# Hybrid attention, GLA and Hyena block, fp32 on one core: the adaLN projection leaves the weight ring

## The chip, the cores and the metric

One of the eight cores of a Trainium2 chip runs the kernel. The metric is the time of one execution on the device in microseconds (us); the median of three runs stands for a kernel. TensorE is the matrix engine, VectorE and ScalarE the elementwise engines, GpSimd (POOL) and SyncE (SP) mostly issue DMAs here. The page of the profile calls them PE, DVE, ACT, POOL and SP.

## The reference

Two layers of a diffusion backbone in fp32, 256 latent and 256 context tokens, width 1024. What bears on this case is how a layer gets its modulation: from a conditioning vector (c for the latents, c_ctx for the context) six vectors of 1024 are made, with a weight w_ada of 1024 x 6144 per layer and a bias b_ada:

```
mod = silu(c) @ w_ada[layer] + b_ada[layer]        # for c and for c_ctx
shift1, scale1, gate1, shift2, scale2, gate2 = split(mod, 6)
h   = layer_norm(x) * (1 + scale1) + shift1
y   = token_mixer(h)                    # differential attention, GLA, Hyena, gates, output projection
x   = layer_norm(ALPHA * x + gate1 * y) * ln1_g + ln1_b
h   = layer_norm(x) * (1 + scale2) + shift2
x   = layer_norm(ALPHA * x + gate2 * conv_ffn(h)) * ln2_g + ln2_b
```

Layer 1, the last, needs the context only as keys, values and GLA state, so its gate1, shift2, scale2 and gate2 are wanted for the latents alone. Only the latents are put out.

## The kernel before, in words

All weights pass through one ring of four buffers (NBUF): SP loads a chunk of 512 KB (256 rows of K by 512 columns) into `stage` (L517 to L521), ScalarE rounds it to `w_hi` (L1073), VectorE makes `w_lo`, the rest (L1418), and TensorE multiplies three times with operands of 128x128 by up to 512 columns in the fp32r format: hi by hi, lo by hi, hi by lo (`three`, L696). The split runs AHEAD = 3 chunks in front of TensorE's use. A chunk has 24 matmuls in most groups.

The order of all this is one list of steps written by `plan()` (L158). Each engine walks through the same list and does its part of each step, so each engine's queue is in that order. A `group` is a projection in 1, 2, 4 or 11 chunks (a_q, a_k, a_v, three of hy, g_v, g_qk, z, six of gate, g_r, six of branch, two of out, two of down); other steps (an attention unit, a Hyena or GLA piece) are put between its chunks from lists of slots. The up projection is a hardware loop of 11 times four chunks.

The adaLN projection is a set of groups too (turn "A"): 12 per layer, each 512 columns wide with four chunks. Its stationary operand is `ada_c`, 128 columns of which four are used: silu(c) and silu(c_ctx), each as hi and lo; so a chunk has four matmuls of 128x128 by 512 columns (`ada_chunk`, L744). The first four groups of layer 0 (shift1, scale1) are the first thing that the kernel does; the other eight of layer 0 lie between the chunks of g_r, gate and branch (2 ada chunks after each); the twelve of layer 1 lie in the down projection of layer 0 (3, later 2 after each). ScalarE copies the four rows of a finished group to `mod_row` (L1170), POOL writes them to DRAM (`d_mod`), and reads them back as rows of 128 (`modload`), VectorE adds hi, lo and bias (L1474, L1475), TensorE turns them to columns (`modcols`, L761), and ScalarE copies them out, so that `modulate` (L1150) can use them as per-partition scale and bias. The gates are written to DRAM once more (`d_gate`) and broadcast from there to all 128 partitions (`gate_rows`, POOL), for the residual (L1608).

At the start ScalarE's queue issues the loads of x, VectorE makes the moments of the layer norm, ScalarE normalises (L1136), TensorE transposes (L772), and ScalarE and VectorE modulate and split the result to `h_hi` and `h_lo`.

The attention mix has one unit per chunk (`attend`, from hy on): TensorE scores, VectorE the maxima (L1666), ScalarE the exponentials (L1263), VectorE the reciprocals and the difference of the two maps (L1670 to L1673), TensorE the transposes (L886) and the product with the values. After four units come `head_norm` and a transpose (`y_turn`, L905). Banks 0 to 3 of PSUM belong to the chunks of a group, banks 4 to 7 to what lies between.

Of the kernel before, what the change touches and what calls it, by code (L numbers as in the profile page):

```python
# [14 lines left out]
P = 128  # L26
D = 1024
# [91 lines left out]
ADA_GROUPS = (range(0, 4), range(4, 12))  # L119
# [23 lines left out]
class Group:  # L143


    def __init__(self, kind, layer, index, turn, n_chunks, tiles, bank0=0, pair=False):
# [4 lines left out]
        self.late = pair or kind in ("a_q", "a_k", "a_v", "hy", "g_v", "g_qk") or self.key == ("ada", 0, 3)  # L151
# [3 lines left out]

def plan():  # L158
# [14 lines left out]
    def ada(layer, groups, bank0=4):  # L173

        out = []
        for i in groups:
            g = Group("ada", layer, i, "A", 4, [i % 2], bank0)
            out += [[("chunk", g, j)] for j in range(4)]
            out[-1].append(("evac", g))
        return out  # L180

    def spread(slots, chunks, first, per):

        for n, item in enumerate(chunks):
            slots[first + n // per] += item

    steps += [("start",), ("modbias", 0, 0)]
    slots = ada(0, ADA_GROUPS[0])
    for tt in range(4):
        slots[9 + tt].append(("moments", 0, 0, tt))  # L190
    steps += sum(slots, [])
    steps += [("modload", 0, 0), ("params", 0)]
    steps += [("deviation", 0, 0, tt) for tt in range(4)] + [("normal", 0, 0, tt) for tt in range(4)]
    steps += [("turn", 0, 0, 0), ("modcols", 0, 0), ("turn", 0, 0, 1)]
    steps += [("modulate", 0, 0, s, b) for b in range(4) for s in range(2)]
    for layer in range(DEPTH):
# [4 lines left out]
        if last:  # L201
            filt[0] += [("modulate", layer, 0, 0, b) for b in range(4)]
            filt[8].append(("modcols", layer, 1))
        else:
            filt[1].append(("consts",))
# [37 lines left out]
        for tt in qt:  # L243
            mix += [[("gla_out", layer, tt)]]
        for j in range(5):
            group("gate", layer, j, "F", 4, range(4), mix)
# [6 lines left out]
        if not last:  # L253
            slots[0].append(("modbias", layer, 1))
            spread(slots, ada(layer, ADA_GROUPS[1]), 0, 2)
            slots[15].append(("modload", layer, 1))

# [9 lines left out]
        slots = [[], [("modcols", layer, 1)] if not last else [], [("gate_rows", layer, 0)], [],  # L267
# [6 lines left out]
        slots[8] += [("gate_rows", layer, 1), ("residual", layer, 1)]  # L274
        if not last:

            slots[0].append(("modbias", layer + 1, 0))
            spread(slots, ada(layer + 1, range(0, 8)), 0, 3)
            slots[6].append(("modload", layer + 1, 0))
            slots[8].append(("modcols", layer + 1, 0))  # L280
# [1610 lines left out]
```

## Time and profile before

| | |
|---|---|
| three runs | 1848.07, 1854.63, 1859.21 us; median 1854.63 |
| profiled execution, first to last instruction (span) | 1850.7 us, of the same size as the runs |
| TensorE busy | 1657.6 us (90%) |
| VectorE busy | 1055.1 us (57%) |
| ScalarE busy | 866.0 us (47%) |
| granted clock of TensorE, mean | 0.946 of 2.4 GHz |
| loads of w_ada | 96 of 512 KB, of 252 MB in all |

The span has no measured part around it, so the profiled execution is compared by its span. How to read the rows: "busy" is the union of an engine's instructions in the stretch, "(x...)" their count; PEclk is the clock that TensorE was granted, 1.00 for 2.4 GHz and 0.50 for 1.2 GHz. Matmuls overlap: a row gives 0.39 us for one of 128x128 by 512 columns, while the next starts much earlier, so the distance of two starts is the price of one in a row of them. "[2.27 <-DVE w_lo L1418]" says that the engine had been idle for 2.27 us until that instruction's result came. Operands are named as out<-moving,stationary. An fp32 matmul (not fp32r) stands in the trace as two records.

### The profile page before, as it was taken

What the parts mean: (1) busy time and instruction counts of PE and PEld (TensorE: products, weight loads), DVE (VectorE), ACT (ScalarE), POOL (GpSimd) and SP (SyncE); (2) the same over time, 40 slices, a digit from 0 to 9 for tenths busy, and PEclk for the clock granted to TensorE, in tenths of its full rate; (3) what the DMA queues carried; (4) which work ended last, traced back from release to release, by engine and by line L of the source; (5) the groups of instructions that cost most, each with busy time, mean ns of one, the idle gap of its engine ahead of it and who ended that gap; (6) DMA issues with size and microseconds to landing.
All of it is one profiled execution on the core that took longest, in us unless ns stands there. A gap on an engine that the chain in (4) does not pass through costs nothing. (4 is left out here: it accounts for less than half of the span.)

```text
span 1850.7 us, 23144 instructions
## 1 busy us (share of the span) xinstructions
PE 1657.6 (90%) x8523; PEld 1364.9 (74%) x8523; DVE 1055.1 (57%) x1609; ACT 866.0 (47%) x1242; POOL 106.9 (6%) x204
## 2 busy tenths in 40 slices
PE   5899899999799996999999989599898878879995
PEld 3777667777687775788887767477786777769984
DVE  6545663523364668566566554865634345778864
ACT  5524543155355424545545434634534644457741
POOL 0200000000001110000000000300000001100000
PEclk8899999999789998999999989799899989989998
DMA  8422113233146772322335856422232335745572
GB/s 307 135 68 80 58 46 91 70 102 103 47 144 221 255 260 91 103 91 91 91 107 179 292 191 211 143 88 73 92 114 80 114 92 173 243 134 181 187 241 68
DMA packets 147909, 252.46 MB, mean 136 GB/s; under 512 B 11842, under 2 KB 59900, under 8 KB 147568
## 3 DMA queue, kind: packets, MB, share of 16 engines
q1 hardware_dynamic: 135472, 216.77, 37.1%
q0 software_dynamic: 11776, 32.45, 5.2%
q10 hardware_dynamic: 576, 2.10, 0.3%
q8 instruction: 55, 0.90, 0.2%
q14 instruction: 30, 0.25, 0.0%
HBM read 235.28 MB, written 15.99 MB: 136 GB/s over the span
## 5 line engine op out<-in xcount | busy, mean ns | idle before, releaser
L1418 DVE TENSOR_TENSOR w_lo<-stage,w_hi 128x1024 fp32r<-128x1024 f32 x302 | 362.4, 1222 | 342.6 <-ACT w_hi L1073 341.1
L689 PE MATMUL ps<-h_hi,w_hi 128*128 128x512 f32 (+1 forms) x1360 | 472.4, 347 | 8.4 <-ACT sig L1220 4.7
L689 PE MATMUL ps<-h_lo,w_hi 128*128 128x512 f32 (+1 forms) x1360 | 462.7, 340 | 0.0
L689 PE MATMUL ps<-h_hi,w_lo 128*128 128x512 f32 (+1 forms) x1360 | 462.7, 340 | 0.0
L1073 ACT ACTIVATE w_hi<-stage 128x1024 fp32r<-128x1024 f32 x302 | 312.6, 1055 | 315.0 <-PE ps L689 243.4
L689 PEld LDWEIGHTS ps<-h_hi,w_hi 128*128 128x128 f32 x1360 | 261.3, 192 | 41.9 <-issue 8.2
L689 PEld LDWEIGHTS ps<-h_hi,w_lo 128*128 128x128 f32 x1360 | 261.3, 192 | 27.6 <-issue 0.7
L689 PEld LDWEIGHTS ps<-h_lo,w_hi 128*128 128x128 f32 x1360 | 260.8, 192 | 28.0
L689 PE MATMUL ps<-w_hi,h_hi 128*128 128x512 f32 x384 | 156.0, 406 | 9.6 <-DVE w_lo L1418 4.3
L1819 DVE TENSOR_TENSOR w_lo<-stage,w_hi 128x1024 fp32r<-128x1024 f32 x88 | 104.5, 1223 | 86.1 <-ACT w_hi L1367 85.4
L689 PE MATMUL ps<-w_lo,h_hi 128*128 128x512 f32 x384 | 152.8, 398 | 0.0
L689 PE MATMUL ps<-w_hi,h_lo 128*128 128x512 f32 x384 | 152.8, 398 | 0.0
L1367 ACT ACTIVATE w_hi<-stage 128x1024 fp32r<-128x1024 f32 x88 | 89.1, 1052 | 76.9 <-PE ps L689 74.5
L689 PE MATMUL ps<-w_hi,act_hi 128*128 128x512 f32 x264 | 106.5, 403 | 4.1 <-DVE ffn_t L1832 3.3
L1832 DVE SCALAR_TENSOR_TENSOR ffn_t<-ps,pcol,ffn_t 128x510 f32<-128x510 f32 (+1 forms) x176 | 95.7, 609 | 25.1 <-ACT ffn_t L1374 23.9
L689 PE MATMUL ps<-w_hi,act_lo 128*128 128x512 f32 x264 | 105.7, 400 | 0.0
L689 PE MATMUL ps<-w_lo,act_hi 128*128 128x512 f32 x264 | 105.5, 400 | 0.0
L689 PE MATMUL ps<-w_hi,ada_c 128*128 128x512 f32 x192 | 83.1, 433 | 22.7 <-DVE w_lo L1418 22.7
L689 PEld LDWEIGHTS ps<-w_hi,h_hi 128*128 128x128 f32 x384 | 74.3, 193 | 31.2 <-issue 8.7
L689 PEld LDWEIGHTS ps<-w_lo,h_hi 128*128 128x128 f32 x384 | 73.9, 192 | 16.0
L689 PEld LDWEIGHTS ps<-w_hi,h_lo 128*128 128x128 f32 x384 | 74.1, 193 | 15.4 <-issue 0.5
L689 PE MATMUL ps<-w_lo,ada_c 128*128 128x512 f32 x192 | 80.6, 420 | 0.0
(262 smaller groups left out, 2124.9 us busy)
## 6 DMA issues: line engine op xcount, KB each, us to landing
stage<-in_w_in SPq DMA_DIRECT2D x122, 512.0 KB
stage<-in_w_ada SPq DMA_DIRECT2D x96, 512.0 KB
stage<-in_ffn_w_up SPq DMA_DIRECT2D x176, 256.0 KB
stage<-in_ffn_w_down SPq DMA_DIRECT2D x44, 512.0 KB
stage<-in_w_branch SPq DMA_DIRECT2D x24, 512.0 KB
stage<-in_w_out SPq DMA_DIRECT2D x16, 512.0 KB
d_sig<-sig POOLq DMA_DIRECT2D x24, 256.0 KB, 3.1
sig_in<-d_sig POOLq DMA_DIRECT2D x24, 256.0 KB, 5.3
```

What stands on the lines that cost most here:

```text
L689: return pe.matmul(out_, lhsT, rhs, start=start, stop=stop, skip_group_check=True)
L1073: act.activation(w_hi[:, s, :], stage[:, s, :], ACT.Copy).then_inc(sem("hi_ready"), 1)
L1367: act.activation(w_hi[:, s, :], stage[:, s, :], ACT.Copy).then_inc(sem("hi_ready"), 1)
L1418: dve.tensor_tensor(w_lo[:, s, :], stage[:, s, :], w_hi[:, s, :].bitcast(F32), ALU.subtract)\
L1819: dve.tensor_tensor(w_lo[:, s, :], stage[:, s, :], w_hi[:, s, :].bitcast(F32), ALU.subtract)\
L1832: dve.scalar_tensor_tensor(out=dst[:, :, to], in0=src[:, :, of], scalar=col, in1=dst[:, :, to], op0=ALU.mult, op1=ALU.add)\
```

## The change

The adaLN projection no longer goes through the ring.

- Layer 0's shift1 and scale1: SP loads all of their weight (8 x 2 tiles of 128 x 1024, 8 MB) into SBUF that is free at the start, and TensorE multiplies in plain fp32 with the weight as the stationary operand and two columns (silu(c), silu(c_ctx)) as the moving one: 128 matmuls (`first_ada`), six of eight K steps ahead of the first half of the transposes, the other two behind it. VectorE adds the bias (`first_mod`). The first two weight chunks are split (`presplit`) just ahead of the modulation.
- The other 20 groups (8 of layer 0, 12 of layer 1): per K tile a load of 128 x 512 (256 KB, SP's queue) into a ring of four tiles, and on VectorE one multiply-accumulate per vector (`ada`): `acc += w * c[k]` with a per-partition scalar; two vectors, but one for layer 1 from group 4 on. 160 tiles. Then TensorE sums over the partitions by fp32 matmuls with a column of ones and adds the bias with the identity (`ada_sum`), and ScalarE copies the columns (`ada_cols`).
- `with_ada` puts these steps into the list by chunk number: five runs, from chunk 9 at 1.75 tiles per chunk, from 43 at 1.3, from 125 at 1.5, from 160 at 1.75, from 187 at 1.1. Without the ada groups the chunks are: a_q, a_k, a_v 0 to 11, hy 12 to 23, g_v, g_qk, z 24 to 32, gate 33 to 52, g_r 53, gate 57, branch 61, out 73 to 80, up 81 to 124, down 125 to 146, and layer 1 in the same order from 147 on. SP waits, ahead of a tile's load, for the use of the tile four before.
- Gate rows: VectorE multiplies the identity by the gate's columns (`diag`, 128 x 1024), TensorE multiplies it by a matrix of ones (two fp32 matmuls of 512 columns), and ScalarE copies the two banks.
- DRAM is out of all this: `d_mod` and `d_gate` go, and POOL's steps with them. In layer 1 dft and idft are loaded again (the ring of tiles has used their place). The conditioning vectors and b_ada come in as one set of rows.

```diff
+ADA_RUNS = ([(0, q) for q in range(4, 9)], [(0, 9), (0, 10), (0, 11), (1, 0)], [(1, q) for q in range(1, 4)],
+            [(1, q) for q in range(4, 8)], [(1, q) for q in range(8, 12)])
+ADA_SLOTS = ((9, 1.75), (43, 1.3), (125, 1.5), (160, 1.75), (187, 1.1))
+ADA_RING = 4
...
+def with_ada(steps):
+    begin, finish, n = {}, {}, 0
+    for run, groups in enumerate(ADA_RUNS):
+        first, per = ADA_SLOTS[run]
+        for i, (layer, q, k) in enumerate([(*who, k) for who in groups for k in range(KT)]):
+            c = first + int(i / per)
+            early = 80 if run == 2 else first
+            at_ = early if i < ADA_RING else c + 4
+            begin.setdefault(at_, []).extend(([("ada_open", run)] if i == 0 else []) + [("ada_load", n)])
+            finish.setdefault(c, []).append(("ada", n))
+            if k == KT - 1:
+                begin.setdefault(c + 1, []).extend([("ada_sum", layer, q), ("ada_cols", layer, q)])
+            n += 1
...
-    steps += [("start",), ("modbias", 0, 0)]
-    slots = ada(0, ADA_GROUPS[0])
...
+    steps += [("first_ada", k) for k in range(6)] + [("turn", 0, 0, 0)] + [("first_ada", k) for k in range(6, KT)]
+    steps += [("first_mod",), ("turn", 0, 0, 1), ("presplit",)]
...
+                elif st[0] == "ada_load":
+                    n = st[1]
+                    layer, q, k = ada_who(n)
+                    if n >= ADA_RING:
+                        sp.wait_ge(sem("ada_done"), at("ada_done", *ada_who(n - ADA_RING)))
+                    sp.dma_start(ada_tile(n), A["w_ada"][layer, k * P:(k + 1) * P, q * COLS:(q + 1) * COLS])\
+                        .then_inc(sem(f"ada_in{n % ADA_RING}"), 16)
...
+            def first_ada(k):
...
+                cv = c_act[:].rearrange("p (v k) -> p k v", v=2)[:, k, :]
+                for w in (1, 0):
...
+                    for n in range(KT):
+                        o = 2 * (w * KT + n)
+                        ins = mm(ps[:, 3, o:o + 2], src[:, n * P:(n + 1) * P], cv, start=(k, w, n) == (0, 1, 0), stop=k == KT - 1)
...
+            def ada_sum(layer, q):
+                b = ada_bank(layer, q)
+                pe.wait_ge(sem("ada_done"), at("ada_done", layer, q, KT - 1))
+                claim(b)
+                acc_ = ada_acc(ADA_ORDER.index((layer, q)))
+                for v in ada_vecs(layer, q):
+                    for n in range(4):
+                        mm(ps[:, b, 4 * v + n:4 * v + n + 1], acc_[:, v, n * P:(n + 1) * P], ones[:, 0:1], start=(v, n) == (0, 0), stop=False)
+                    ins = mm(ps[:, b, 4 * v:4 * v + 4], ident[:], b_col[:, layer, q // 2, q % 2 * 4:q % 2 * 4 + 4], start=False)
+                full(ins, b, "ada", layer, q)
+
+            def gate_rows(layer, which, v):
+                pe.wait_ge(sem("diag"), at("diag", layer, which, v))
+                for half in range(2):
+                    b = 4 + 2 * v + half
+                    claim(b)
+                    full(mm(ps[:, b, :], ones[:], diag[which][:, 4 * half:4 * half + 4, :].rearrange("p k n -> p (k n)")),
+                         b, "gates", layer, which, v)
...
+            def ada(n):
+                layer, q, k = ada_who(n)
+                m, w = n // KT, ada_tile(n)
+                dve.wait_ge(sem(f"ada_in{n % ADA_RING}"), 16 * (n // ADA_RING + 1))
...
+                for v in ada_vecs(layer, q):
+                    col, acc_ = c_act[:, KT * v + k:KT * v + k + 1], ada_acc(m)[:, v, :]
+                    if k == 0:
+                        ins = dve.tensor_scalar(acc_, w, col, None, ALU.mult)
+                    else:
+                        ins = dve.scalar_tensor_tensor(out=acc_, in0=w, scalar=col, in1=acc_, op0=ALU.mult, op1=ALU.add)
+                do(ins, "ada_done", layer, q, k)
```

## Rows read from the trace of the kernel before

**Rows 1.** The page, parts 1 and 5: busy us by engine; the split on VectorE, mean ns.
```profile
PE 1657.6 (90%) x8523; PEld 1364.9 (74%) x8523; DVE 1055.1 (57%) x1609; ACT 866.0 (47%) x1242; POOL 106.9 (6%) x204
...
L1418 DVE TENSOR_TENSOR w_lo<-stage,w_hi 128x1024 fp32r<-128x1024 f32 x302 | 362.4, 1222 | 342.6 <-ACT w_hi L1073 341.1
```

**Rows 2.** Busy time by stretch: span, its length, engines' busy us, clock, DMA share, GB/s.
```profile
0.00:57.45 57.45, 31.48 (x98) 22.48 (x99) 32.90 (x52) 32.09 (x41) 10.76 (x25) 0.76 0.81 276
161.00:272.00 111.00, 102.59 (x492) 77.45 (x491) 72.91 (x134) 55.78 (x108) 0.00 (x0) 0.97 0.20 60
...
513.90:672.30 158.40, 149.11 (x625) 118.71 (x625) 101.65 (x119) 75.68 (x94) 20.31 (x38) 0.96 0.65 213
...
976.00:1168.30 192.30, 178.00 (x742) 141.23 (x740) 106.96 (x112) 82.34 (x94) 10.43 (x20) 0.96 0.64 215
1269.00:1331.00 62.00, 51.43 (x340) 42.12 (x339) 44.00 (x79) 32.89 (x63) 0.00 (x0) 0.92 0.27 77
```

**Rows 3.** Timeline of TensorE: start us, own length; eight matmuls apart, then five.
```profile
528.75 0.39 PE L689 MATMUL ps<-w_hi,ada_c 128*128 128x512 f32 x1
...
530.56 0.39 PE L689 MATMUL ps<-w_hi,h_hi 128*128 128x512 f32 x1
...
1024.78 0.40 PE L689 MATMUL ps<-w_hi,act_hi 128*128 128x512 f32 x1
...
1025.95 0.40 PE L689 MATMUL ps<-w_lo,act_hi 128*128 128x512 f32 x1
```

**Rows 4.** Stretches, the instructions that touch ada_c alone (four matmuls per chunk).
```profile
513.90:672.30 158.40, 34.67 (x128) 24.32 (x128) 0.00 (x0) 0.00 (x0) 0.96 0.65 213
976.00:1168.30 192.30, 48.75 (x192) 37.03 (x192) 0.00 (x0) 0.00 (x0) 0.96 0.64 215
```

**Rows 5.** Timeline of TensorE in the down projection of layer 0.
```profile
1057.91 0.79 PE L689 MATMUL ps<-w_hi,ada_c 128*128 128x512 f32 x1 [2.27 <-DVE w_lo L1418]
...
1071.62 0.31 PE L761 MATMUL ps<-ident,mrows 32*128 32x32 f32 x1 [9.27 <-DVE mrows L1475]
```

**Rows 6.** Groups by shape (busy, mean ns), then the timeline: fp32 matmuls on TensorE.
```profile
L689 PE MATMUL ps<-v_tok,attT 128*128 128x128 f32 x160 | 21.8, 275 | 1.4 <-DVE y_tok L1691 1.4
...
160.66 0.61 PE L689 MATMUL ps<-v_tok,attT 128*128 128x128 f32 x4
...
111.00 3.17 PE L689 MATMUL ps<-f_sd,dft 128*128 128x512 f32 x7
```

**Rows 7.** Timeline of VectorE: a dependent pair and the next, independent one.
```profile
163.82 0.74 DVE L1523 SCALAR_TENSOR_TENSOR x0T<-ps,pcol,x0T 128x510 f32<-128x510 f32 x1
164.60 0.75 DVE L1526 SCALAR_TENSOR_TENSOR x0T<-ps,pcol,x0T 128x510 f32<-128x510 f32 x1
165.26 0.74 DVE L1523 SCALAR_TENSOR_TENSOR x0T<-ps,pcol,x0T 128x510 f32<-128x510 f32 x1
```

**Rows 8.** Waits of VectorE in 161 to 272 us: total, times, longest.
```profile
DVE soft L1670 <- ACT probs L1263: 18.0, 13, 1.6
DVE soft L1666 <- PE ps L689: 13.1, 5, 7.7
```

**Rows 9.** Waits of VectorE in 1266 to 1340 us, the longest.
```profile
DVE soft L1670 <- ACT probs L1263: 12.7, 8, 1.6
```

**Rows 10.** Timeline of the start: last w_ada chunk, transposes, first matmul of a_q.
```profile
34.54 1.06 ACT L1073 ACTIVATE w_hi<-stage 128x1024 fp32r<-128x1024 f32 x1 [1.42 <-DMA stage<-in_w_ada]
...
48.32 3.65 PE L772 MATMUL ps<-ident,xn_mix 128*128 128x128 f32 x16 [5.09 <-ACT xn_mix L1136]
...
57.45 0.47 PE L689 MATMUL ps<-w_hi,h_hi 128*128 128x512 f32 x1 [0.30 <-issue]
```

**Rows 11.** Stretches, all engines: GLA output products, and transposes ahead of a_q.
```profile
508.00:511.40 3.40, 3.40 (x34) 3.40 (x32) 1.53 (x3) 0.56 (x1) 0.00 (x0) 0.50 0.00 0
511.40:514.85 3.45, 3.45 (x22) 3.02 (x20) 2.57 (x6) 0.63 (x3) 0.00 (x0) 0.50 0.00 0
...
54.06:57.46 3.40, 3.10 (x16) 2.72 (x14) 2.21 (x4) 2.92 (x6) 3.40 (x8) 0.50 0.61 81
```

More of the change, by code:

```diff
@@ L171, in group @@
             steps.extend(between.pop(0))
[L173 to L185, printed above, removed]
-    steps += [("start",), ("modbias", 0, 0)]
-    slots = ada(0, ADA_GROUPS[0])
[L189 to L192, printed above, removed]
+    steps += [("start",)]
+    steps += [("moments", 0, 0, tt) for tt in range(4)]
+    steps += [("params", 0)]
     steps += [("deviation", 0, 0, tt) for tt in range(4)] + [("normal", 0, 0, tt) for tt in range(4)]
-    steps += [("turn", 0, 0, 0), ("modcols", 0, 0), ("turn", 0, 0, 1)]
+    steps += [("first_ada", k) for k in range(6)] + [("turn", 0, 0, 0)] + [("first_ada", k) for k in range(6, KT)]
+    steps += [("first_mod",), ("turn", 0, 0, 1), ("presplit",)]
     steps += [("modulate", 0, 0, s, b) for b in range(4) for s in range(2)]
@@ L244, in plan @@
             mix += [[("gla_out", layer, tt)]]
+        if last:
+            mix += [[] for _ in range(20 - len(mix))]
         for j in range(5):
@@ L642, in chunk @@
                         dma(sig_in[:, n, o:TOK], d_sig[g.layer][8 * br + 4 * half + n, :, o:TOK], f"sig_in{n}", g.layer, g.index)
-            def gate_rows(layer, which):
-                what = ("branch", layer, (1, 2)) if which == 0 else ("base", "up end", layer)
-                pool.wait_ge(sem("bank_full3"), at("bank_full3", *what))
-                pool.wait_ge(sem("gate_out"), 16 * at("gate_out", layer))
-                for s in range(tok0(layer) // SEQ, 2):
-                    v = 1 - s
-                    dma(R[which]["g"][:, v, :], bc(d_gate[layer][v, 3 * which * D:(3 * which + 1) * D], D), f"gates_in{s}", layer, which)
             def post(layer, which, tt):
@@ L807, in chunk @@
                                         h_hi[:, k, :], h_lo[:, k, :], k == 0, k == KT - 1)
-                    for kk in range(2 if g.turn not in "AZ" else 0):
+                    for kk in range(2 if g.turn != "Z" else 0):
                         k = 2 * j + kk
@@ L1457, in params_turn, with gate_rows @@
+            def gate_rows(layer, which, v):
+                for q in (4 + 6 * which, 5 + 6 * which):
+                    freed(ada_bank(layer, q), "ada", layer, q)
+                if v:
+                    for half in range(2):
+                        bank(4 + half, "gates", layer, which, 0)
+                col = mod[:, layer, 2 + 3 * which, v, :]
+                do(dve.tensor_tensor(diag[which][:], wide(ident[:], KT), wide(col, P, 2), ALU.mult), "diag", layer, which, v)
             def params_turn(layer):
```

292 lines of the change are left out of this document (137 added, 155 removed).

## Prediction

> **What bounds the kernel now.** I read the page's engine totals first: TensorE is busy 1657.6 of the 1850.7 us span, VectorE 1055.1, ScalarE 866.0 [rows 1]. Only what shortens TensorE's queue, or makes it wait, shows in the time. Then I read the table by stretch [rows 2]: TensorE has only 31.48 us of work in the 57.45 us start, and it idles where two other things end last: in the attention mix (161 to 272 us, 102.59 busy) and in the two stretches in which w_ada passes through the weight ring (149.11 of 158.40 and 178.00 of 192.30). The span is my base; the median of the runs, 1854.63, lies 3.9 us above it, and I add the change to the median.
>
> **What is taken away.** Each w_ada chunk in the ring costs TensorE four matmuls that start 0.227 us apart [rows 3], so 0.91 us. Eighty of the 96 chunks lie after the start: 32 in 513.9 to 672.3 (29 us) and 48 in 976 to 1168.3 (44 us) [rows 4]. They also shorten the ring's lead, which is three chunks: an ada chunk covers 0.91 us, a normal one (24 matmuls) 5.45. The splits that go with them (1222 ns each on VectorE [rows 1], about as much on ScalarE) are off the path there. The bytes stay: 80 loads of 512 KB become 160 of 256 KB; of POOL's, the round trips through d_mod and d_gate and six 512 KB gate broadcasts go.
>
> *Layer 0, 513.9 to 672.3.* What remains is 20 chunks x 24 matmuls x 0.229 us = 110 us (0.227 in the first eight chunks, a little more in the branches), 3 us of small transposes and cold matmuls, 6 us of waits (today 9.3 us of the stretch are idle [rows 2], and the shorter ring lead makes some of that), and 7 us of new sums (below): 126. For the first branch chunks VectorE will be about full (two chunks: 5.5 us evacuation, 2.4 splits, 3.7 new accumulation against 11.1 us of TensorE), so 128. Gain 30; bounds 22 and 35.
>
> *Down projection of layer 0, 976 to 1168.3.* Besides the 44 us the ring stalls here: at 1057.9 TensorE waits for a split, and from 1062 to 1071.6 for the rows of the modulation that come back from DRAM (9.27 us), and around the hole the matmuls last up to 0.79 us in place of 0.40 [rows 3, 5]. Both have no place in the new code. Remaining: 5.7 us of up, 22 x 24 x 0.234 [rows 3] = 123.6, sums 6.6, gate rows 3.4, 2 of waits = 141.3. Gain 51; bounds 45 and 53.
>
> **What is added on TensorE.** An accumulator is summed by four fp32 matmuls with one column plus one with four columns, per vector. An fp32 matmul is two records here (the 80 products of attT are 160 records [rows 6]). No row has a moving operand this narrow; the nearest is 128x128 by 128 columns: four records take 0.61 us and one 0.275, so starts are 0.11 us apart [rows 6]. I take 0.11, because both the load of 128 columns and the stream could set it; half of that is the lower bound. Ten records per vector are 1.1 us. There are 12 groups with two vectors and 8 with one: 32 x 1.1 = 35 us in all, exposed wherever TensorE is the bound: 2.2 in the gla stage of layer 0, the 7 and 6.6 already counted, 1 per group for the eight of layer 1, less two hidden in its attention = 6.4. A gate row pair is two 512-column fp32 matmuls, four records 0.43 us apart ((3.17 - 0.59) / 6, a record of 512 columns at the end being 0.59 [rows 6]) = 1.7 us; two in the out stage of layer 0 (+3.4), one each in out and down of layer 1 (+3.4, against which the broadcast of the gates from DRAM goes: say +3). The VectorE product for them (two inputs of 1024, as the split: 1.2 us) lies under the chunk, as do the small copies on ScalarE (20 of columns, 12 of gate rows at 0.6), whose queue loses 96 splits.
>
> **What is added on VectorE.** 160 tiles of 128x512. The nearest rows are scalar_tensor_tensor with a per-partition scalar, 0.75 us; two that don't depend on each other start 0.66 apart, dependent ones 0.78 [rows 7]. So a tile costs 1.42 us with two vectors and about 0.75 with one. They are spread by chunk number, 1.75 per chunk over the layer-0 attention mix (chunks 9 to 31), 1.3 over gates to branch, 1.5 over down, 1.75 over the layer-1 attention (160 to 178), 1.1 after that. SP's weight loads now also queue behind a wait for the tile four back; the ring's three chunks cover that.
>
> *Layer-0 attention.* VectorE's queue is in order and each attention unit has a hole of 1.2 to 1.6 us in it while ScalarE makes the exponentials. In 161 to 272 it is busy 72.91 us, 18.0 go in those holes and only 13.1 are waits for TensorE, 7.7 of them in one piece [rows 2, 8]. With smaller waits it is occupied some 95 of 111 us. 22.75 tiles x 1.42 = 32.3 more make 127. Two idle pieces stay: about 5 us after the last head norm, and about 6 because TensorE makes the sum (2.2 us, and it waits for the last tile) ahead of the next scores. That is 138 against 111: +27, and the order of the queues allows no catching up. Bounds: +15 (holes closed by overlap with the wait for evacuation) and +38. The five sums here are inside it.
>
> *Layer-1 attention.* Here VectorE is busy 44.00 of 62 us, waits 12.7 for exponentials, and has no wait for TensorE at all [rows 2, 9]: it is the bound already. Nine chunks x 1.75 x 0.75 = +11.8, one hidden sum overshoot: +12. Bounds +8 and +17.
>
> *Elsewhere.* The gla stage of layer 0 gets 1.3 tiles per chunk in a queue with chains in it: +1.3 beside the sum (0 to 5), 3.5 in all. Params of layer 1 now reload dft and idft (1 MB) on POOL's queue ahead of the last small load; 1 MB is 3.8 us at the 276 GB/s of the start [rows 2], and what waits for it comes after a chunk of matmuls: 0, bound +4.
>
> **The start.** The loads are the same size (16 x 512 KB and x); the last w_ada chunk is taken up at 34.5 us and the first real matmul starts at 57.45 [rows 10]. What lies between is ring, DRAM round trip, and transposes. New: 128 fp32 matmuls with two columns, 256 records, after a first load that lands near 7 us (an estimate: two loads' worth of bytes at the rate of [rows 2], and the issue). Their price is 0.11 us at 2.4 GHz; at 1.2 GHz the sixteen transposes in 3.65 us give 0.22 (they are at the lower clock; (3.65 - 0.4) / 15) [rows 10], so I take 0.213, two cycles of 1.2 GHz for each of 128 columns. So 28 us, hidden under the loads, or 55 us, which is not. Which clock they get decides. In 508.0 to 511.4 TensorE is busy all 3.40 us with 64x64 products and the granted clock is 0.50, and in 511.4 to 514.85 it is so again; in 54.06 to 57.46 it is busy 3.10 us with full 128x128 transposes, and the clock has risen in the matmul that follows, 0.47 us against 0.79 [rows 5, 10, 11]. Two-column products are more like the former than the latter, so I take the lower clock of the two, 1.2 GHz. Then 7 + 55 + 3.4 (turn 0) = 65, the modulation's columns 1, and an estimated 3.4 us to modulate and split the first tiles (today it can begin in 54.06 to 57.46, ahead of the matmul at 57.45 [rows 10, 11]): 70 less a fraction, some +13 against 57.45 (bounds +9, +16). At full clock: 34.5 + 3.4 + 1.7 + 4 = 44, -14.
>
> The Trainium skill, page TensorE: Matmul & The Clock Gate, Part 1, says that the throttled state is the default and activity releases it, without a condition on the shape. By that rule the start comes out at -14, the first rival. The rows at 508.0 to 514.85 speak against it [rows 11].
>
> **Sum.** +13 +27 +3.5 -30 +3.4 -51 +12 +6.4 +3 = about -13; for the sums' waits on ScalarE's copies before the shared bank 6 is free I add 3: -10. 1854.6 - 10 = 1844.6, or 0.54% less. With all bounds drawn together by half: 1832 to 1858.
>
> **The rivals.** (1) Warm start: -14 in place of +13, 1817.6 (1806 to 1830). For it: TensorE would have no gap in the whole of it; against it: [rows 11]. (2) Slower: VectorE's order in the attention mixes costs every tile in full, since slack sits behind ScalarE's exponentials and TensorE's y turns and can't be used. Then layer 0 pays (22.75 + 12) x 1.42 + 6.8 = 56 in place of 27 and layer 1 19 x 1.3 = 25 in place of 12: +42, 1886. It decides from some 19 us beyond my forecast on. For it: in 161 to 272 the idle time is one piece of 7.7 us and small ones; against: the tiles of chunks 9 to 14 and 28 to 31 lie where VectorE is idle half of the time. (3) The ring's stalls don't go away (sig and branch loads set them) and only the matmuls' own time returns: 8 us less gain, 1853.
>
> **Chances.** Forecast 0.50, warm start 0.30, VectorE in full 0.12, stalls stay 0.08. What a measurement can tell from no change is about 0.5%, 9 us: faster means under 1845.4. The forecast straddles that (0.26 faster, 0.21 same, 0.03 slower); warm start gives 0.29 and 0.01; (2) 0.01 same, 0.11 slower; (3) 0.01, 0.06, 0.01. Faster 0.56, same 0.29, slower 0.15. The range takes in the warm start and stops in the lower half of (2): 1804 to 1866.
>
> **What would show it.** First real matmul at 70 us and granted clock 0.5 from 7 to 65 (or 44 and 1.0); records of the two-column products 0.21 or 0.11 apart; the stretch from the first scores to the q/k projection of gla 27 us longer with hardly any wait of VectorE for TensorE; down of layer 0 near 136 us with no hole; VectorE near 1120 us busy, ScalarE near 770. The prediction is wrong if narrow fp32 records cost something else than 0.11, if the clock drops inside the stages for the new sums, or if SP's new waits starve the ring.

## The result and the profile after

The changed kernel takes 1879.11 us (median of four runs, 1878.13 to 1882.28) against 1851.35 before (four runs): a ratio of 1.0149 with a 95% interval of 1.0120 to 1.0178. It is slower by about 28 us, where 10 us less was forecast, and it lies outside the range of 1804 to 1866. The profiled execution has a span of 1880.5 us against 1850.7, so the two traces differ by 29.8 us. Three executions in all the sets below, one of e1 (2744.85 us) and two of the kernel before, were slow ones, far above all others, and are left out of the ratios.

The page after, part 1. It answers to the first of [rows 1]:

```profile
PE 1690.6 (90%) x8735; PEld 1410.4 (75%) x8735; DVE 1110.5 (59%) x1766; ACT 767.0 (41%) x1151; POOL 82.4 (4%) x158
```

The engines' totals are as forecast (VectorE near 1120, ScalarE near 770). TensorE is busy 33 us longer, though 73 us of ring matmuls (by the distance of their starts) have gone: new narrow products, and more time at 1.2 GHz. So the table by stretch is next. The columns are those of [rows 2]; the stretches are cut at the same matmuls (the first one, the chunk that began at 161 and the one at 272, g_r to branch, down of layer 0 from 976 on, the attention of layer 1).

```profile
0.00:74.34 74.34, 61.98 (x289) 61.41 (x290) 12.58 (x36) 14.57 (x21) 11.78 (x26) 1.00 0.65 227
179.64:329.25 149.61, 123.57 (x556) 94.02 (x554) 103.54 (x181) 56.35 (x114) 0.00 (x0) 0.87 0.27 87
583.29:717.72 134.43, 129.53 (x558) 105.68 (x557) 90.79 (x127) 40.59 (x57) 15.01 (x28) 0.93 0.50 157
1024.10:1171.60 147.50, 143.85 (x617) 114.73 (x615) 83.45 (x111) 32.10 (x41) 0.00 (x0) 0.97 0.41 136
1270.00:1339.50 69.50, 56.73 (x353) 46.48 (x352) 51.68 (x93) 32.49 (x64) 0.00 (x0) 0.90 0.36 109
```

The second line is the loss: 149.6 us where 111.0 to 111.4 stood. The third and the fourth are the gains, 24 and 45 us. The 1.00 of the first line is no reading: this trace's first clock record is a rise at 77.7 us, and ahead of it the distances of the matmuls tell the clock.

Cut into stages that add up, the two spans differ so (us; the stages are named by what TensorE begins with):

| stage | before | after | difference | forecast |
|---|---|---|---|---|
| start, to the first weight matmul | 57.4 | 74.3 | +16.9 | +13 |
| a_q, a_k, a_v | 84.0 | 83.6 | -0.4 | 0 |
| attention mix of layer 0, to z | 162.0 | 205.0 | +43.1 | +27 |
| gates and GLA of layer 0 | 210.5 | 220.3 | +9.8 | +3.5 |
| g_r to branch of layer 0 | 158.5 | 134.4 | -24.1 | -30 |
| out and norms | 67.1 | 69.9 | +2.8 | +3.4 |
| up | 244.8 | 244.7 | 0 | 0 |
| down of layer 0 and norms | 207.2 | 161.6 | -45.7 | -51 |
| a_q to a_v of layer 1 | 74.4 | 72.4 | -2.0 | 0 |
| attention mix of layer 1 | 73.5 | 85.7 | +12.1 | +12 |
| the rest of layer 1 | 511.4 | 528.6 | +17.2 | +12.4 |

The last cell of the forecast is 6.4 for sums, 3 for gate rows and the 3 for bank 6. Every stage that was forecast to change went the way that was said. The attention mix of layer 0 misses by 16 us, and five other stages by 4 to 6 each, to the same side; all together it is 39.5 us.

Waits in the attention mix of layer 0, 157.9 to 348.8 us of the trace after (engine, line and tile, what it waited for, total, times, longest), VectorE's and then TensorE's; they answer to [rows 8]:

```profile
DVE soft L1697 <- ACT probs L1256: 21.9, 16, 1.6
DVE soft L1693 <- PE ps L698: 16.9, 5, 7.7
DVE vvT L1548 <- ACT vvT L1195: 8.5, 1, 8.5
...
PE ps L899 <- ACT attT L1261: 14.8, 3, 6.9
PE ps L698 <- DVE acc_c L1479: 4.9, 1, 4.9
```

The holes behind the exponentials are as long as before (21.9 us in 16), as forecast. But VectorE still waits 16.9 us for TensorE's scores, where the forecast had hardly any such wait, so it is not full all the time; the wait for vvT has grown from 3.1 to 8.5 us; and TensorE stands 4.9 us ahead of one sum. The experiments start from these rows.

### The profile page after: what moved, and what is told of

Same layout as the page of the kernel before. It is cut to its first block and busy times, and to the rows that moved or that the text cites. A ratio compares the mean times of both kernels' runs of the same rounds, so it can differ in the third digit from the quotient of the medians.

```text
span 1880.5 us, 23778 instructions
## 1 busy us (share of the span) xinstructions
PE 1690.6 (90%) x8735; PEld 1410.4 (75%) x8735; DVE 1110.5 (59%) x1766; ACT 767.0 (41%) x1151; POOL 82.4 (4%) x158
## 5 line engine op out<-in xcount | busy, mean ns | idle before, releaser
L698 PE MATMUL ps<-h_hi,w_hi 128*128 128x512 f32 (+1 forms) x1360 | 476.9, 351 | 12.4 <-ACT sig L1216 5.8
L1411 DVE TENSOR_TENSOR w_lo<-stage,w_hi 128x1024 fp32r<-128x1024 f32 x206 | 249.5, 1222 | 254.7 <-ACT w_hi L1067 254.3
L1067 ACT ACTIVATE w_hi<-stage 128x1024 fp32r<-128x1024 f32 x206 | 215.3, 1058 | 267.2 <-PE ps L698 245.2
L1846 DVE TENSOR_TENSOR w_lo<-stage,w_hi 128x1024 fp32r<-128x1024 f32 x88 | 104.6, 1223 | 86.9 <-ACT w_hi L1360 86.1
L698 PE MATMUL ps<-w_hi,h_lo 128*128 128x512 f32 x384 | 153.1, 399 | 0.0
L1360 ACT ACTIVATE w_hi<-stage 128x1024 fp32r<-128x1024 f32 x88 | 89.1, 1051 | 77.7 <-PE ps L698 77.6
L698 PE MATMUL ps<-ys_hi,w_hi 128*128 128x512 f32 (+1 forms) x192 | 71.0, 370 | 8.2 <-ACT sig L1216 4.2
L594 POOL DMA_DIRECT2D d_sig<-sig x48 | 26.1, 545 | 972.9 <-ACT sig L1216 972.3
```

What stands on the lines that cost most here:

```text
L594: pool.dma_start(dst, src, allow_slow_non_contiguous=True).then_inc(sem(stage_), 16 * tick(stage_, *who))
L698: return pe.matmul(out_, lhsT, rhs, start=start, stop=stop, skip_group_check=True)
L1067: act.activation(w_hi[:, s, :], stage[:, s, :], ACT.Copy).then_inc(sem("hi_ready"), 1)
L1360: act.activation(w_hi[:, s, :], stage[:, s, :], ACT.Copy).then_inc(sem("hi_ready"), 1)
L1411: dve.tensor_tensor(w_lo[:, s, :], stage[:, s, :], w_hi[:, s, :].bitcast(F32), ALU.subtract)\
L1846: dve.tensor_tensor(w_lo[:, s, :], stage[:, s, :], w_hi[:, s, :].bitcast(F32), ALU.subtract)\
```

## The experiments

Each kernel ran beside the kernel before on the same chip, so times are compared by their ratio to it (with its 95% interval; it isn't exactly the quotient of the medians). The kernel before had medians of 1851.28, 1851.35 and 1851.55 us in the three sets. "Attention" is, in all of them, the stretch from the first hyena chunk to the last transpose of the attention's output: 150.0 us before, 190.9 us after. The start is the least steady stretch: with the same code it ended at 70.8 to 74.3 us in nine profiles, and differences under 4 us of the whole are not read. Other stretches differ too with the same code in them: the attention took 188.2 to 190.9 us in four traces, gates and GLA of layer 0 220.3 to 226.3 in seven, g_r to branch 131.2 to 137.9 in seven, down and norms 160.1 to 162.3 in seven. Each kernel has one trace, so a difference by place counts where it is beyond these.

### What the products on VectorE cost (e1)

```diff
                     bank(7, "filter", layer, 3)
+                if k and ada_run(m) == 0:
+                    dve.sem_inc(sem("ada_done"), 1)
+                    tick("ada_done", layer, q, k)
+                    return
                 for v in ada_vecs(layer, q):
```

> The changed kernel, but of the 40 w_ada tiles of the first run (chunks 9 to 31, the layer-0 attention mix) only the first product of each of the five groups is made; the other 35 are left out, while their loads, the signals and the five sums on TensorE stay. Theory V (VectorE pays every tile in full in the attention mix, which is full already): 35 x 1.42 us = 50 us of work go and the stretch from the first hyena chunk to the first gate chunk falls from 205.0 us to 165 or a little under (it was 161.95 before the change), the whole by about 40 us, to 1839. Rival S (the sums on TensorE and what waits behind them make the stretch longer): only the waits for the last tile of a group go, 9 us in this stretch, so 1870. Rival L (SyncE's waits for the tiles delay the weight loads): nothing goes but what VectorE's later signals held up, under 5 us.

Measured: 1858.72 us (median without the one at 2744.85), ratio 1.0032 (1.0012 to 1.0051), 20 us less than the changed kernel. The attention takes 167.3 us, 23.6 less. The 35 tiles are some 50 us of work, but some of them lie ahead of this stretch, in a_v, which is no shorter without them (83.6 us in both), and some behind it; inside it VectorE is busy 33.9 us less. So a tile in the attention costs some 70% of its own time, and the tiles of the run together less than half. Theories V and S are each right in part, and rival L (under 5 us) is out. The load of VectorE reaches TensorE ahead of the transposes of the attention's output too: its waits there (L899 after, L905 before) were 7.8 us before, 14.8 after, and are 6.7 here. The other 17 us of the loss are there without the products. The table by stretch, the attention before:

```profile
141.40:291.40 150.00, 141.59 (x680) 108.69 (x680) 91.26 (x164) 72.19 (x136) 0.00 (x0) 0.98 0.23 67
```

The same after:

```profile
157.90:348.80 190.90, 164.86 (x760) 127.72 (x759) 128.76 (x224) 72.15 (x140) 0.00 (x0) 0.89 0.29 91
```

And in this kernel:

```profile
157.70:325.00 167.30, 158.23 (x761) 123.26 (x760) 94.89 (x172) 72.23 (x140) 0.00 (x0) 0.93 0.34 106
```

VectorE has nearly the load of before (94.9 against 91.3 us), and TensorE is busy 16.6 us longer than before: now the sums are in the way.

### What the sums on TensorE cost (e6, e9)

```diff
                 acc_ = ada_acc(ADA_ORDER.index((layer, q)))
+                if ada_run(ADA_ORDER.index((layer, q))) == 0:
+                    full(mm(ps[:, b, 0:8], ident[:], ones[:, 0:8]), b, "ada", layer, q)
+                    return
                 for v in ada_vecs(layer, q):
```

> The changed kernel, but each of the five sums of the first run (after chunks 14, 18, 23, 27 and 32) is one product of two records in place of 20; 18 records of each are left out, while the waits for the accumulator, the copies on ScalarE and VectorE's products stay. Theory T (TensorE's own time for the sums is exposed in the attention mix): 5 x 18 x 0.11 = 10 us less, a little more where the clock is at its lower level, 1867. Rival V (VectorE is the bound of this stretch): TensorE waits in their place, 1 to 4 us less, 1876.

Measured: 1857.67 us, ratio 1.0039 (1.0014 to 1.0064), 21 us less than the changed kernel in the median, where 12 were expected. In the traces it is 18.0 less: the attention has 12.6 (178.3 us; four of the five sums are in it), the part of its stage behind it 2.0 (the fifth sum), and the start, whose code is the same, 3.5. Theory T stands: 14.6 us for 90 records is 0.16 us per record, more than the 0.11 of a record at 2.4 GHz.

```diff
                 for v in ada_vecs(layer, q):
-                    for n in range(4):
-                        mm(ps[:, b, 4 * v + n:4 * v + n + 1], acc_[:, v, n * P:(n + 1) * P], ones[:, 0:1], start=(v, n) == (0, 0), stop=False)
-                    ins = mm(ps[:, b, 4 * v:4 * v + 4], ident[:], b_col[...], start=False)
+                    ins = mm(ps[:, b, 4 * v:4 * v + 4], ident[:], b_col[...], start=v == 0)
```

> The changed kernel, but every sum keeps only the product with the bias columns: the four products that sum an accumulator over the partitions are left out (8 of 10 records per vector, 256 records in all); waits, copies and VectorE's products stay. Theory T (the sums' own time on TensorE is exposed wherever they stand): 256 x 0.11 = 28 us less at least; by the run with short sums in the first run only (12.6 us of the attention mix for 90 vector records more than nothing, 1.26 us per vector) up to 36: 1843 to 1851, with 4 us of it between the attention and g_r of layer 0, 5 in g_r to branch, 6 in down, 8 to 10 in layer 1. Rival W (VectorE is late with the accumulators, and TensorE would wait in the place of the sums): outside the attention mixes nothing, 1864.

Measured: 1843.72 us, ratio 0.9967 (0.9953 to 0.9982): 35 us less, where 28 was the price of the 256 records at 0.11 us. Rival W is out. By place: attention 12.0, g_r to branch 8.1 (126.3 against 134.4), down and norms 7.8 (156.3 against 164.1, counted from down's first matmul), gates and GLA only 0.5, the attention mix of layer 1 3.1 (82.5 against 85.7) and the rest of layer 1 4.0, where 8 to 10 were expected for that layer. Without these products the change would have been a gain of 0.3%. The 28 was too low because some of the sums run at 1.2 GHz: in the trace after six of the 20 do so in whole or in part (3.4 to 4.3 us in place of 2.3, and one of a single vector 2.1 in place of 1.2), 8.4 us more in all. TensorE waits for the last tile ahead of eight of the 20 sums, 20.6 us in all. One of these in the trace after, in the GLA stage (timeline of TensorE; start, length, idle time ahead):

```profile
514.43 1.71 PE L698 MATMUL ps<-ones,acc_c 128*128 128x1 f32 x8 [2.91 <-DVE acc_c L1479]
516.01 0.57 PE L698 MATMUL ps<-b_col,ident 128*128 128x4 f32 x2
516.43 1.85 PE L698 MATMUL ps<-ones,acc_c 128*128 128x1 f32 x8
518.14 0.57 PE L698 MATMUL ps<-b_col,ident 128*128 128x4 f32 x2
518.64 2.07 PE L698 MATMUL ps<-w_gate,zT 33*128 33x512 f32 x2
```

TensorE waits 2.9 us for the last tile, then the records of one column are 0.21 us apart at the lower clock ((1.85 - 0.35) / 7), 4.3 us in all; elsewhere, at 2.4 GHz, a sum of two vectors takes 2.3 us. The forecast had 2.2 for it here, and 1.3 for whatever else the tiles do in this stage.

### What stands behind a sum: ScalarE's copy (e5, e2)

```diff
         out.append(st)
+        if st[0] == "evac":
+            out += held
+            held = []
         if st[0] == "chunk":
             out += begin.get(c, [])
+            if st[2] == st[1].n - 1:
+                held = sums.get(c, [])
+            else:
+                out += sums.get(c, [])
```

> The changed kernel with one thing moved: where a sum stands behind the last chunk of a group, the sum and the copy of its columns come behind that group's evacuation in the order of the steps (five sums: behind chunks 23, 27, 32, 174, 178). TensorE's order of work stays almost the same, ScalarE's changes. Theory O (the copy, which waits for the sum, holds up ScalarE's evacuation of the last hyena group: VectorE waits 8.5 us for vvT there against 3.1 before the change, and that unit lasts 23.9 us against 16.4): the unit gets 6 us shorter, three later places 1 us each, 9 us less in all, 1870. Rival V (VectorE's sum of work sets that unit's length, the copy was hidden by it): within 2 us of the changed kernel, 1878.

Measured: 1872.06 us, ratio 1.0115 (1.0098 to 1.0132), 7 us less than the changed kernel; the attention takes 182.2 us, 8.7 less, and the unit after the last hyena chunk (from VectorE's first score maximum to the next unit's) 16.7 us in place of 23.9. VectorE's wait for vvT there is 1.2 us in place of 8.5. Theory O. ScalarE's timeline in the trace after shows it:

```profile
274.25 0.18 ACT L1102 ACTIVATE mod<-ps 128x8 f32<-128x8 f32 x1 [9.11 <-PE ps L698]
274.32 1.44 ACT L1195 ACTIVATE vvT<-ps,pcol 128x512 f32<-128x512 f32 x2
```

The copy of 0.18 us waits 9.1 us for the sum, which comes when all four banks of the group are done. The evacuation behind it, which could have begun with the first bank, waits too. The forecast had 3 us in the whole kernel for what waits on these copies, and did not see that ScalarE's queue has work behind them.

```diff
-                begin.setdefault(c + 1, []).extend([("ada_sum", layer, q), ("ada_cols", layer, q)])
+                sums.setdefault(c + 1, []).extend([("ada_sum", layer, q), ("ada_cols", layer, q)])
...
         if st[0] == "chunk":
-            out += finish.get(c - 1, [])
+            out += sums.get(c - 1, []) + finish.get(c - 1, [])
```

> The changed kernel with each sum of an accumulator, and the copy of its columns, put just before the next chunk, that is behind the chunk's evacuation and its other steps, in place of right behind the chunk. In the changed kernel's trace TensorE stands still ahead of the sums for 21 us in all, 9 of them in the two attention mixes of layer 0 and 6 in that of layer 1, and 1 us behind three sums at a group's end, where ScalarE copies the columns before it empties the banks. Theory V: the waits in the attention mixes come from VectorE being full and only move; outside them the waits go, 3.1 + 2.7 + 2.0 + 1.9 + 0.6 and some 3 us of evacuation: 13 us less, 1866. Rival S: all of it goes, 25 us less, 1854.

Measured: 1885.68 us, ratio 1.0186 (1.0160 to 1.0211), 7 us more than the changed kernel in the median (the intervals of the ratios overlap), where 13 or 25 less was expected; both theories are wrong. The attention takes 197.0 us, 6.1 more. The unit of the last hyena chunk is back at 16.9 us, and the next one has gone from 9.7 to 17.0. Its timeline (lines left out), TensorE, ScalarE and VectorE:

```profile
278.65 1.84 PE L698 MATMUL ps<-ones,acc_mix 128*128 128x1 f32 x8 [5.62 <-ACT attT L1261]
...
282.91 0.77 PE L698 MATMUL ps<-w_hi,h_hi 128*128 128x512 f32 x1
...
283.09 0.18 ACT L1102 ACTIVATE mod<-ps 128x8 f32<-128x8 f32 x1 [4.58 <-PE ps L698]
283.16 2.00 ACT L1067 ACTIVATE w_hi<-stage 128x1024 fp32r<-128x1024 f32 x2
...
284.25 1.23 DVE L1411 TENSOR_TENSOR w_lo<-stage,w_hi 128x1024 fp32r<-128x1024 f32 x1 [1.61 <-ACT w_hi L1067]
```

TensorE stands 5.6 us ahead of this sum (9.5 us ahead of three of them) until ScalarE has copied attT: the sum and the transposed probabilities use the same PSUM bank, number 6, and that copy stands behind the next unit's exponentials in ScalarE's queue. Then the copy of the sum has the next weight splits behind it in that queue, and VectorE's split waits 1.6 us for them. What a sum in a bank of its own would do was not tried. The Trainium skill says (page TensorE: Matmul & The Clock Gate, Part 1, Architectural detail) that the queues of ScalarE and VectorE are strictly first in, first out, while TensorE's can pull weight loads ahead. Both runs agree with the first half.

### What can be hidden (e3, e8)

```diff
                 do(dve.tensor_scalar(s[:, 2:4], s[:, 0:2], -0.125, ...), "neg_max", layer, i)
+                if tile is not None:
+                    ada(tile)
                 for m in range(2):
                     freed(4 + m, "scores", layer, i)
```

> The changed kernel with one w_ada tile of each attention unit moved on VectorE's queue into the unit, between the negated maximum and the reciprocal, where VectorE waits 1.2 to 1.6 us for ScalarE's exponentials; the same products, the same chunks. Theory V with the holes free: 16 units of layer 0 save 1.37 us each (21.9 us of such waits in the trace), 8 units of layer 1 save 0.75 us: 22 + 6 = 28 us less, 1851. Rival: the units are bound by the chain scores, maximum, exponentials, difference, transpose, and not by VectorE's sum of work; then a tile in the hole saves nothing, and where it reaches past the exponentials it adds, 0 to +5 us.

Measured: 1858.26 us, ratio 1.0041 (1.0024 to 1.0058), 21 us less than the changed kernel; the attention of layer 0 172.0 us (18.9 less for 22.7 us of tiles), that of layer 1 75.4 against 81.2. One unit in VectorE's timeline:

```profile
232.22 0.17 DVE L1694 TENSOR_SCALAR soft<-soft 128x2 f32<-128x2 f32 x1
232.30 1.41 DVE L1479 SCALAR_TENSOR_TENSOR acc_mix<-ada_y,c_act,acc_mix 128x512 f32<-128x512 f32 x2
233.97 0.17 DVE L1699 RECIPROCAL soft<-soft 128x2 f32<-128x2 f32 x1 [0.26 <-ACT probs L1256]
```

The tile of 1.41 us lies in the hole, and 0.26 us of wait are left. The forecast said that these holes can't be used by this order of the queue; that is right, and the order that can use them is one step of the list away.

```diff
-ADA_SLOTS = ((9, 1.75), (43, 1.3), (125, 1.5), (160, 1.75), (187, 1.1))
+ADA_SLOTS = ((3, 0), (43, 1.3), (125, 1.5), (150, 0), (187, 1.1))
+ADA_AT = {0: [3 + (i * 9) // 16 for i in range(16)] + list(range(12, 28)) + [28, 29, 29, 30, 30, 31, 31, 32],
+          3: [150 + (i * 3) // 4 for i in range(12)] + list(range(159, 167)) + [167 + (i * 7) // 12 for i in range(12)]}
```

> The changed kernel with the w_ada tiles of both attention runs laid out by hand: in layer 0 16 tiles go to chunks 3 to 11, ahead of the attention mix, one to each of the 16 units (in its wait for the exponentials), 8 behind it; in layer 1 12, 8 and 12 in the same way. The accumulators change roles, so that the one that is free first is used first. Theory V (a tile costs its time only where VectorE is full, and moved to where TensorE is the bound it costs nothing): against the changed kernel 28 us from the holes as before, of which the run with one tile in each hole has shown 21, and 16 tiles less in the queue, another 8 to 15; the sums' cost stays; 1845 to 1850. Rival: VectorE becomes late for a_k and a_v (its splits queue behind tiles), and what the attention gives is lost there: 1858 or more.

Besides the diff it has the tile in the unit as in e3, and `acc_c` serves the even groups in place of the odd. Measured: 1850.54 us, ratio 0.9994 (0.9982 to 1.0007). The attention takes 158.3 us, but a_q to a_v takes 92.1 in place of 83.6: TensorE waits 2.6 us for the first accumulator behind a_k, makes the sum (2.7 us), and makes the filter's products after it at the lower clock (granted 0.50 from 131.7 to 138.6 us). So the rival holds in part.

### The later products (e10)

```diff
                     bank(7, "filter", layer, 3)
+                if k and ada_run(m) != 0:
+                    dve.sem_inc(sem("ada_done"), 1)
+                    tick("ada_done", layer, q, k)
+                    return
                 for v in ada_vecs(layer, q):
```

> The changed kernel, but in runs 2 to 5 of the w_ada tiles (all but the first run) only the first product of each group is made; 105 of 120 tiles are left out of VectorE's queue, 70 us with two vectors and 42 with one. Theory V' (outside the attention mixes VectorE's work is hidden; only TensorE's waits ahead of sums whose last tile is late go, 11 us in layer 0 and 7 in layer 1, and in layer 1's attention mix half of its 14 tiles' time, 5 us): 18 to 23 us less, 1859. Rival O (all of it is hidden and the waits come from somewhere else): 5 us less, 1874.

Measured: 1857.64 us, ratio 1.0034 (1.0020 to 1.0048), 21 us less. Theory V' by the total. By place it is 10.8 in g_r to branch of layer 0, 8.9 of it in the branch chunks (74.8 us against 83.7); 8.5 in the attention of layer 1 (72.7 against 81.2, more than expected, for 10.2 us less of VectorE's busy time), 2.3 in down. VectorE is not free of charge in the branches: 4.4 of the 10.8 us are TensorE's waits ahead of two sums (2.6 and 1.8), the rest is spread.

### The start (e4, e7)

```diff
                     for n in range(KT):
                         ... two-column products
+                    mm(ps[:, 7 if k < 6 else 0, :], ident[:], src[:, 0:512])
```

> The changed kernel with 15 extra fp32 products of 128x128 by 512 columns in the start, one behind every eight two-column products, into a bank that nobody reads. Theory N (the two-column products ran at 1.2 GHz because of their shape, and wide products among them raise the clock): their records go from 0.213 to 0.11 us apart, 28 us for all, the fillers cost 15 x 0.86 = 13 us, and the first weight chunk starts some 12 us earlier, near 62: 1867. Rival C (the start is at the lower clock whatever runs in it, or 0.213 is the price of the shape): the records stay 0.213 apart and the fillers cost 15 x 1.71 = 26 us at the lower clock, 1905, or 13 us at the higher, 1892.

Measured: 1901.40 us, ratio 1.0266 (1.0249 to 1.0283); the first weight matmul stands at 96.5 us, 22 to 26 later. Rival C, at the lower clock. This trace has clock records in the start; the timeline of TensorE:

```profile
82.69 3.41 PE L698 MATMUL ps<-c_act,ada_sc 128*128 128x2 f32 x16
85.96 2.06 PE L698 MATMUL ps<-ada_sc,ident 128*128 128x512 f32 x2
```

And the stretch from 79.8 to 92 us, all engines:

```profile
79.80:92.00 12.20, 12.20 (x47) 10.13 (x48) 0.56 (x5) 0.11 (x1) 0.00 (x0) 0.50 0.00 0
```

TensorE is busy in all of the 12.2 us, with one wide product behind every sixteen narrow records, and is granted 0.50. The first clock record is a rise at 76.3 us, and ahead of it the narrow records are 0.213 us apart. So over the whole start the clock was at its upper level once, from 76.3 to 79.8 us, and it fell with no gap in TensorE's work.

```diff
-                        ins = mm(ps[:, 3, o:o + 2], src[:, n * P:(n + 1) * P], cv, ...)
+                        ins = mm(ps[0:2, b, :], cv, src[:, half * COLS:half * COLS + COLS], ...)
```

> The changed kernel with the operands of the first part exchanged: the two columns of c are the stationary operand and each block of w_ada moves as 512 columns; 32 fp32 products (64 records) give two rows of 2048, which are copied and turned by 16 small transposes. Theory N (the two-column products kept TensorE at 1.2 GHz; 512-column products in a row raise the clock, as the ring's w_ada chunks did before the change): the records are 0.43 us apart, 28 us in all, hidden under the loads, and the first weight chunk starts near 48, 26 us earlier: 1853. Rival C (it stays at the lower clock): 64 x 0.86 = 55 us, and the added copies and transposes put the first chunk at 77: 1882.

Measured: 1863.05 us, ratio 1.0070 (1.0053 to 1.0087), 16 us less than the changed kernel; the first weight matmul stands at 48.3 us, 23 to 26 earlier. In the trace gates and GLA are longer (212.8 against 208.5 us from the first hyena transform on; 226.3 against 220.3 for the whole stage, the upper end of what the same code took). Timeline of TensorE:

```profile
11.06 3.21 PE L699 MATMUL ps<-ada_sc,c_act 128*2 128x512 f32 x4 [2.12 <-DMA ada_sc<-in_w_ada]
14.11 1.88 PE L699 MATMUL ps<-ada_sh,c_act 128*2 128x512 f32 x4
```

And the stretch from 10 to 39.5 us:

```profile
10.00:39.50 29.50, 28.44 (x64) 5.51 (x64) 2.88 (x13) 8.95 (x14) 11.56 (x22) 1.00 1.04 360
```

The first four records are 0.8 us apart, the next four 0.43 ((1.88 - 0.59) / 3); the trace's clock record is a rise at 13.8 us. Theory N. In the changed kernel the two-column records are 0.213 us apart over 58 us, in which TensorE is busy 57.7. Two operands changed places, the multiplications are the same, and the clock is at its other level. The shape alone would gain nothing: at the 0.8 us of the first four, 64 records take 51 us (an estimate), against the 55 us of 256 narrow ones.

### The parts together (e11)

```diff
+                if (layer, q) != (0, 9):
+                    sums.setdefault({(0, 4): 10}.get((layer, q), c + 1), []).extend([("ada_sum", layer, q), ("ada_cols", layer, q)])
...
+        if st == ("gla_scan", 0):
+            out += [("ada_sum", 0, 9), ("ada_cols", 0, 9)]
```

> A version made of the parts that have helped: the wide start (512 columns of w_ada move, the columns of c are stationary), the tiles laid out by hand with one in each attention unit's wait for the exponentials, sums and column copies behind a group's evacuation, the sum for the first group three chunks later (TensorE waited 3 us for it behind a_k), that for the sixth behind the gla states, where TensorE waits for VectorE anyway. If the parts add up: 1850.5 for the spread version, -26 for the start, -5 for the sum behind a_k, -5 for that in the gla stage, -2 in layer 1: 1813, 2% faster than before the change. Rival: the stages are coupled (a clock that falls elsewhere, VectorE later in a_q after the earlier start) and give back half: 1830.

Measured: 1807.65 us (1806.06 to 1811.90), ratio 0.9774 with an interval of 0.9752 to 0.9796: 2.3% faster than before the change. Besides the diff it has the wide start, the layout of e8 and the order of e5. The parts add up: start 48.9 us, a_q to a_v 85.9, attention 158.2, gates and GLA 199.9 against 208.5 after and 198.7 before (from the first hyena transform on). The page's part 1:

```profile
PE 1641.7 (91%) x8559; PEld 1345.5 (75%) x8559; DVE 1110.3 (61%) x1768; ACT 769.6 (43%) x1153; POOL 82.7 (5%) x158
```

VectorE and ScalarE have the load of the changed kernel to 3 us. What differs is where in the queues it stands, the shape of the first products, and TensorE's clock.

## Why the prediction was wrong

**The start: right, with its reason.** +13 was forecast (bounds +9 to +16) from the lower clock and 0.213 us per record; it is +13 to +17, with records 0.213 us apart. The warm start did not come. The rows of 64x64 products [rows 11] spoke for narrow work at 1.2 GHz; e7 and e4 show it by changing the shape. What the forecast took from the Trainium skill (page TensorE: Matmul & The Clock Gate, Part 1) as the rival, that activity releases the throttle, holds for the 512-column products of e7 and did not for the two-column ones.

**The attention mix of layer 0: the step that failed.** It said +27, with bounds +15 to +38, for the stretch of 111 us, which is +38 to +39, and put nothing outside it, where there are 4.8. Its working was: VectorE at 127 us of work, "about 6 because TensorE makes the sum", and the five sums inside. The runs show three costs there. The products are worth 23.6 us in the attention (e1); the forecast, 27 less the 6 of the sum, had 21 for them, so this term was near, though VectorE was not full as it said (16.9 us of waits for scores and 8.5 for vvT are left). The sums' own matmuls are worth 12.6 (e6), where 6 was allowed for the sum and its wait. The copy's place ahead of an evacuation is worth 8.7 (e5; at least 6.0 by the spread of this stretch), where nothing was. (They overlap by 4: their sum is 45, the loss 41.) So the sum was mis-sized by half, and the copy was a term put at nothing. The forecast named "if the clock drops inside the stages for the new sums" as a sign of being wrong, and this one came: TensorE was at 1.2 GHz for 41.0 of the 190.9 us, against 6.8 of 150.0 before and 23.9 of 167.3 in e1.

**Branch, down, gates of layer 0: smaller misses.** 1.1 us per vector was right as TensorE's own time at 2.4 GHz: ten records 0.11 apart, from the fp32 rows of 128 columns [rows 6]. In g_r to branch the sums gave back 8.1 us (e9) where 7 was in the forecast; the late products cost 10.8 (e10), waits ahead of sums included, where 2 was. So VectorE's load there is the term that was too low. In the gates the wait for the last tile (2.9 us) and the sum at the lower clock (4.3) are seen, but without the products of the sums the stage is only 0.5 us shorter, and in e11, which has the sum behind the states and other changes too, it is 8.6 shorter: that points to the sum's place, and the split of these 9.8 us stays open.

**The gains: right in kind.** The hole at 1057.9 to 1071.6 [rows 5] is gone, and down takes 147.5 us against 192.3 [rows 2] where 141.3 was said. The gain of 45 us is 5 to 6 short. The sums' products give back 7.8 (6.6 had been counted) and the late products 2.3, which leaves part of it unexplained.

**Layer 1: right for the attention, low for the rest.** +12.1 against +12. In the rest 17.2 against 12.4: the sums' products are 4.0 of it (e9) and the late products 4.6 (e10), and no run shows what the other half is.

**The rivals.** The warm start did not come, and the ring's stalls went away: the hole is gone, and g_r to branch has no wait for a split left (4.8 us before). "VectorE in full" gave 1886, 7 us from the result, on the losing side as it said. But its mechanism is only in part what happened: it put 49 us on the tiles of layer 0, and they are worth 23.6; and the attention of layer 1 lost 12 us, not 25. It had the size by putting on the products what the sums and the copies cost, so its nearness is luck. The chance of 0.15 for slower was too low, since three small unknowns (waits ahead of sums, copies, branch load) were each taken at their low end and all pointed the same way. The working's own bounds, drawn together by half, reach some 20 us up (to 1865, and not 1858), and the result lies beyond that too.

**What stays open.** How much of a sum's cost is the lower clock and how much is the wait was not separated by a run. An estimate for the attention: TensorE is busy 23.3 us longer there than before (164.9 against 141.6), e6 takes 11.8 of that away (153.1), and the other 11.5 would be the same matmuls at the lower clock. Of the 23 to 26 us that e7 gains in the start, the whole keeps 16 in the median; where the rest goes was not tried.

## What to carry to other kernels

When work moves from one engine to another, look at the signal that brings its result back: each sum here cost its own time, and, depending on its place, a wait for its last input and a copy on a third engine with that engine's work queued behind it. Price a new step by all queues that it stands in, and place its last, small instruction where nothing that others wait for is behind it. And find the wait that an engine has in every round: work put into that wait is nearly free (18.9 of 22.7 us came back); one step later in the same queue it had cost five sixths of its time.

## What the runs showed of the hardware

- With two columns moving, TensorE stayed at 1.2 GHz for 58 us in which it was busy 57.7; one 512-column fp32 product among sixteen narrow records did not change it (0.50 from 79.8 to 92 us, 12.2 of 12.2 us busy), and a rise at 76.3 us lasted 3.4 us. With the operands exchanged it rose at 13.8 us and stayed up to the end of these products; the first had begun at 11.1.
- An fp32 record with 128x128 weights and 1, 2 or 4 moving columns starts 0.11 us after the last at 2.4 GHz and 0.213 at 1.2 GHz; one with 128 columns, 0.112 and 0.213. At these four widths the width is not what is paid for.
- At equal load of VectorE and ScalarE (to 3 us) the kernel takes 1879 or 1808 us (after and e11).
